# mLSTM gates as eight columns of the value projection, x's mean square per token, and a new order of loads and S5 phases in a decoder layer

## The reference, cut to what matters

```python
def rms_norm(x, g):
    y = xf * lax.rsqrt(jnp.mean(xf * xf, axis=-1, keepdims=True) + RMS_EPS)
    return y * g

p = rms_norm(x, norm_pre_mix) @ w_in     # columns: S5 256 | mLSTM 4*256 + 8 | RWKV 1024 | MoBA 768

# mlstm_mixer
q, k, v, o, i_pre, f_pre = split_cols(p, (GW, GW, GW, GW, nh, nh))     # i_pre, f_pre: 4 + 4 columns
log_i = i_pre + i_bias
bcum = cumsum(log_sigmoid(f_pre + f_bias))    # within a chunk
...
# s5_mixer: diagonal complex recurrence, its phases are cos and sin of t * angle
# cross-attention: memory is normed by its own mean square
```

## Time and profile before

| | |
|---|---|
| median of 3 runs | 482.74 us |
| the profiled execution | 482.97 us, its span (first to last instruction) 481.2 us |
| PE busy | 471.1 us (98%), 3330 matmuls |
| VectorE busy | 345.4 us (72%), 488 instructions |
| ScalarE busy | 270.6 us (56%), 442 instructions |
| GpSimd busy | 108.4 us (23%), 75 instructions |
| chain that ended last | PE 70%, VectorE 19%, issue 3%, ScalarE 3%, DMA 2% |
| granted PE clock | 0.998 of full speed |

### The profile page before, as it was taken

One profiled execution on the slowest core, in us unless ns is written; L12 is line 12 of the kernel. 1 busy time (PEld: TensorE's weight loads), 2 busy tenths in 40 slices (PEclk: granted clock), 3 DMA queues, 4 the chain that ended last, 5 costly groups with the idle time before them and its releaser, 6 DMA issues.

```text
span 481.2 us, 8231 instructions
## 1 busy us (share of the span) xinstructions
PE 471.1 (98%) x3330; PEld 409.0 (85%) x3330; DVE 345.4 (72%) x488; ACT 270.6 (56%) x442; POOL 108.4 (23%) x75
## 2 busy tenths in 40 slices
PE   8999999999999999999999999999999999999995
PEld 6999888989888877889998887888888888888884
DVE  3899999999889887888455736767676777642234
ACT  5678884417232347679557556655555555453342
POOL 0005427793576600000000000000000000344450
PEclk9999999999999999999999999999999999999999
DMA  7874429221410226263733532465555455455502
GB/s 267 338 314 168 161 89 340 69 99 50 148 71 20 89 89 262 86 246 123 260 116 133 207 143 88 176 218 185 196 209 198 176 176 185 172 194 217 193 0 87
DMA packets 12697, 78.91 MB, mean 164 GB/s; under 512 B 1487, under 2 KB 2164, under 8 KB 4084
## 3 DMA queue, kind: packets, MB, share of 16 engines
q1 hardware_dynamic: 12660, 78.39, 45.4%
HBM read 77.33 MB, written 1.84 MB: 165 GB/s over the span
## 4 chain that ended last, share of the span: by engine, by line
PE 70%; DVE 19%; issue 3%; ACT 3%; DMA 2%; POOL 1%; SPq 1%; DVEq 0%; ACTq 0%
PE bank L414 69%; DVE we_rest L385 3%; DMA ring<-weights 2%; POOL arena L1166 1%; DVE arena L1742 1%; DVE wm_rest L385 1%; DVE bank L1689 1%; ACT we_high L379 1%; ACT arena L1440 1%; DVE arena L2014 1%; DVE wk_rest L385 1%; DVE h L1945 0%; DVE arena L397 0%; DVE arena L1759 0%; DVE arena L1879 0%
## 5 line engine op out<-in xcount | busy, mean ns | idle before, releaser
L414 PE MATMUL bank<-h,w_high 128*128 128x512 f32 (+1 forms) x392 | 120.4, 372 | 0.0
L379 ACT ACTIVATE w_high<-ring 128x1024 fp32r<-128x1024 f32 x63 | 66.2, 1058 | 62.7 <-PE bank L414 59.2
L385 DVE TENSOR_TENSOR w_rest<-ring,w_high 128x1024 fp32r<-128x1024 f32 x51 | 63.3, 1245 | 49.2 <-ACT w_high L379 49.0
L414 PE MATMUL bank<-h,w_rest 128*128 128x256 f32 x320 | 89.6, 280 | 0.0
L414 PEld LDWEIGHTS bank<-h,w_high 128*128 128x128 f32 x392 | 68.7, 188 | 13.6 <-issue 0.4
L385 POOL TENSOR_TENSOR w_rest<-ring,w_high 128x1024 fp32r<-128x1024 f32 x7 | 16.8, 2400 | 259.5 <-ACT w_high L379 259.5
L414 PEld LDWEIGHTS bank<-h,w_rest 128*128 128x128 f32 x320 | 60.5, 189 | 0.0
L414 PE MATMUL bank<-arena 64*64 64x64 f32 (+8 forms) x794 | 51.3, 253 | 1.6 <-POOL arena L1119 1.1
L385 DVE TENSOR_TENSOR w_rest<-third_slot,w_high 128x1024 fp32r<-128x1024 f32 x27 | 32.7, 1222 | 27.3 <-ACT w_high L379 27.2
L414 PEld LDWEIGHTS bank<-arena 64*64 64x64 f32 (+4 forms) x794 | 42.2, 144 | 11.4 <-issue 3.9
L414 PE MATMUL bank<-h,we_high 128*128 128x256 f32 x256 | 47.2, 287 | 2.1 <-DVE we_rest L385 1.6
(11 more groups left out here) (341 smaller groups left out, 1020.2 us busy)
## 6 DMA issues: line engine op xcount, KB each, us to landing
ring<-weights SPq DMA_DIRECT2D x49, 1024.0 KB, 4.8
third_slot<-weights SPq DMA_DIRECT2D x15, 1024.0 KB, 4.8
gain<-gains SPq DMA_DIRECT2D x3, 512.0 KB, 5.6
cst<-consts SPq DMA_DIRECT2D x1, 1216.0 KB, 8.8
par<-params SPq DMA_DIRECT2D x1, 1168.0 KB, 10.4
kx<-x_t SPq DMA_DIRECT2D x2, 512.0 KB, 5.6
ring<-weights SPq DMA_DIRECT2D x2, 512.0 KB, 6.6
vx<-mem_t SPq DMA_DIRECT2D x1, 1024.0 KB, 9.7
```

The lines of the kernel that those rows point to most:

```text
L379: nc.scalar.activation(split_half(i)[0], raw_half(i), ACT.Copy).then_inc(S["w_high"], 1)
L385: e.tensor_tensor(rest_, raw_half(i), high.bitcast(F32), ALU.subtract).then_inc(rest_done(i)[0], 1)
L414: return nc.tensor.matmul(out_, lhsT, rhs, start=start, stop=stop, skip_group_check=True)
```

## The change

The 8 gate columns are loaded as a 1024 x 8 matrix, split into high and rest, and stored behind the 256 value columns (`w_gated`); the value product of a token block is 264 columns wide, each block in its own bank. ScalarE copies the 8 columns, scaled, to `gate_cols`, and PE turns them (two transposes) between the halves of ml_o. x's mean square comes from x's rows (tokens on partitions), loaded now before slot 2: two squares with a sum, the root in one column, two diagonal matrices, and PE spreads them over partitions with ones (`rstd_x`). Memory squared follows the shift of rw_v; the sines are built ahead of rests(6); rests(9) and highs(9) go ahead of the theta subtraction and of the shift of rw_r. The identity and time constants join the first constants; the other constants and the later parameters load before slot 6. Nothing else is changed but memory places (Vt and BKt swapped, a memset of `gate_cols`).

```diff
@@ pe @@
+            def values_and_gates(n, names, banks, act):
+                for name, b in zip(names, banks):
+                    pe_open(pe, name, b)
+                pe.wait_ge(S["gate_split"], 4)
+                for j in range(2):
+                    wait_rest(pe, 2 * n + j)
+                    for m in range(2):
+                        o = bank[banks[m]][:, 0:256 + GATES]
+                        for k in range(4):
+                            kt = 4 * j + k
+                            last = mm3(o, [x[:, kt, m * P:(m + 1) * P] for x in act],
+                                       [x[:, k, :] for x in w_gated[j]], kt == 0, kt == KD - 1)
...
             split_channel_major(1, "rw_k", 0, h_split, None, (0,))
-            o = pe_open(pe, "x_sumsq", 2)
-            pe.wait_ge(S["ones_in"], 16)
-            pe.wait_ge(S["x_summed"], 3)
-            mm(o[:, 0:T], const("ones"), sq_x[:, 0, :])
+            o = pe_open(pe, "rstd_x", 2)
+            pe.wait_ge(S["x_diag"], 2)
             for m in range(2):
-                last = mm(o[:, T + m:T + m + 1], sq_x[:, 0, m * P:(m + 1) * P], const("ones")[:, 0:1])
+                last = mm(o[:, m * P:(m + 1) * P], const("ones"), x_diag[:, m, :])
...
-            pe.wait_ge(S["consts_in"], 16)          # before rw_w; now before rw_kk
...
             split_channel_major(6, "ml_k", 1, h_split)
-            o = pe_open(pe, "gates", 2)
-            pe.wait_ge(S["gate_gain"], 1)
-            for k in range(KD):
-                last = mm(o[0:GATES, 0:T], v3(prm("w_gate"), GATES)[:, k, :], hT[:, k, :], k == 0, k == KD - 1)
-            last.then_inc(full[2], 1)
             moved(pe, "s5_u")
+            pe.wait_ge(S["more_params_in"], 16)
...
-            split_values(7, "ml_v", 0, h_split)
-            split_channel_major(8, "ml_o", 1, h_split)
+            values_and_gates(7, ("ml_v0", "ml_v1"), (0, 2), h_split)
+            split_channel_major(8, "ml_o", 1, h_split, None, (0,))
+            o = pe_open(pe, "gates", 7)
+            moved(pe, "ml_v0")
+            moved(pe, "ml_v1")
+            for m in range(2):
+                last = nc.tensor.transpose(o[0:GATE_ROWS, m * P:(m + 1) * P], gate_cols[:, m, 0:GATE_ROWS], const("ident"))
+            last.then_inc(full[7], 1)
+            split_channel_major(8, "ml_o", 1, h_split, None, (1,))
@@ sp @@
                 if n == 2:
                     sp.dma_start(cst[:, 0:CONST_FIRST], consts_d[:, 0:CONST_FIRST]).then_inc(S["ones_in"], 16)
-                if n == 3:
-                    sp.dma_start(cst[:, CONST_MORE:], consts_d[:, CONST_MORE:]).then_inc(S["consts_in"], 16)
+                    for m in range(2):
+                        sp.dma_start(xres[:, m, :], x_rows[m * P:(m + 1) * P, :]).then_inc(S[f"xres{m}_in"], 16)
                 if n == 4:
-                    sp.dma_start(par[:, PARAM_FIRST:], params_d[:, PARAM_FIRST:]).then_inc(S["params_in"], 16)
+                    sp.dma_start(par[:, PARAM_FIRST:PARAM_MORE], params_d[:, PARAM_FIRST:PARAM_MORE]).then_inc(S["params_in"], 16)
...
+                if n == 6:
+                    sp.dma_start(cst[:, CONST_MORE:], consts_d[:, CONST_MORE:]).then_inc(S["consts_in"], 16)
+                    sp.dma_start(par[:, PARAM_MORE:], params_d[:, PARAM_MORE:]).then_inc(S["more_params_in"], 16)
                 if n == S_WKV:
-                    sp.dma_start(xres, x_rows.rearrange("(m p) c -> p m c", p=P)).then_inc(S["xres_in"], 16)
@@ act @@
             highs(2)
-            x_square(0)
+            a.activation(step, prm("log_step"), ACT.Exp).then_inc(S["s5_step"], 1)
             highs(4)
-            x_square(1)
-            a.activation(step, prm("log_step"), ACT.Exp).then_inc(S["s5_step"], 1)
+            for m in range(2):
+                act.wait_ge(S[f"xres{m}_in"], 16)
+                x_square(m)                      # Square of xres[:, m, :] with accum_out=ssq[:, m]
+            a.activation(rstd_col, ssq[:, 0:2], ACT.Ln, bias=const("eps6"), scale=1.0 / D).then_inc(S["sq_ready"], 1)
+            act.wait_ge(S["sq_ready"], 3)
+            a.activation(rstd_col, rstd_col, ACT.Exp, scale=-0.5).then_inc(S["rstd_col"], 1)
+            act.wait_ge(S["rstd_col"], 1)
+            for m in range(2):
+                a.activation(x_diag[:, m, :], const("ident"), ACT.Copy, scale=rstd_col[:, m:m + 1]).then_inc(S["x_diag"], 1)
...
             highs(6)
-            inv_root("x_sumsq", rstd_x, T, 1.0 / D, "eps6").then_inc(S["rstd_x"], 1)
+            a.activation(rstd_x, o[:, 0:T], ACT.Copy).then_inc(free_of("rstd_x"), 1)
...
+            highs(9)
             shifted("rw_r", 2)
             highs(10)
             a.activation(cos, sin, ACT.Abs).then_inc(S["sincos"], 1)
+            shifted("rw_v", 3)
             a.activation(sq_m, mem_h, ACT.Square).then_inc(S["sq_m_ready"], 1)
-            shifted("rw_v", 3)
             highs(12)
+            for j in range(2):
+                a.activation(w_gated[j][0][:, :, 256:256 + GATES], raw_gates(j), ACT.Copy).then_inc(S["gate_split"], 1)
...
-            a.activation(rows[0][0:NH, :], o[32:32 + NH, 0:T], ACT.Identity, bias=prm("f_bias", NH))
...
             highs(H_MID + 2)
-            project_values("ml_v", mlv)
+            gated_values(0, "ml_v0")             # 8 columns to gate_cols, then 256 to mlv, both scaled
+            gated_values(1, "ml_v1")
+            o = wait_full(act, "gates")
+            a.activation(rows[0][0:NH, :], o[32:32 + NH, 0:T], ACT.Identity, bias=prm("f_bias", NH))
@@ dve @@
             rests(4)
-            dve.wait_ge(S["sq_ready"], 2)
-            sum_tiles(dve, v, sq_x, "x_summed")
...
-            rests(6)
-            x_scale("rw_wag")
-            dve.wait_ge(S["consts_in"], 16)
+            dve.wait_ge(S["ones_in"], 16)
             for i in range(8):
                 last = v.tensor_scalar(sin[:, i, :], const("time"), frac[:, i:i + 1], None, ALU.mult)
+            rests(6)
+            x_scale("rw_wag")
...
             x_scale("rw_r")
+            rests(9)
             v.scalar_tensor_tensor(sin, cos, ROUND, sin, ALU.subtract, ALU.subtract).then_inc(S["theta"], 1)
-            rests(9)
...
             rests(12)
-            v.tensor_tensor(w_gate, w_gate, spread(prm("pre_mix"), GATES), ALU.mult).then_inc(S["gate_gain"], 1)
...
             rests(13)
+            for j in range(2):
+                v.tensor_tensor(rest_, raw_gates(j), high.bitcast(F32), ALU.subtract).then_inc(S["gate_split"], 1)
...
-            x_scale("gates", GATES, 1)
...
+            dve.wait_ge(S["consts_in"], 16)      # before the masks of A0 to A7
```

More of the change, by code:

```diff
@@ L23 @@
 DFF = 2816
-GATES = 36
+GATES = 2 * NH
+GATE_ROWS = 36
 NFF = DFF // P
@@ L212, in trunk_kernel @@
             own(stage, "gap", A_AT)
-            w_early = [pair(stage, f"we{i}", HALF, 256) for i in range(HALF_BUFS)]
+            w_early = [pair(stage, f"we{i}", HALF, 256) for i in range(2)]
+            w_gated = [pair(stage, f"we{i}", 4 * (256 + GATES), 256 + GATES) for i in range(2, HALF_BUFS)]
+            w_early += [[x[:, :, 0:256] for x in w] for w in w_gated]
         xtmp = v3(own(ctx, "xtmp", 2 * D), D)
@@ L319, in wait_slot @@
             return slot(n)
-        SCALED = ["rw_wag", "rw_k", "rw_r", "rw_v", "ml_q", "ml_k", "gates", "ml_o"]
+        SCALED = ["rw_wag", "rw_k", "rw_r", "rw_v", "ml_q", "ml_k", "ml_o"]
         def scaled(eng, name):
@@ L483, in split_values @@
                     used(last, i, name if j else None)
+            def values_and_gates(n, names, banks, act):
[3 more added lines that the diff above has]
+                for j in range(2):
+                    i = 2 * n + j
+                    wait_rest(pe, i)
+                    for m in range(2):
[4 more added lines that the diff above has]
+                                       [x[:, k, :] for x in w_gated[j]], kt == 0, kt == KD - 1)
+                        if j == 1 and m == 0:
+                            last.then_inc(full[banks[0]], 1)
+                    used(last, i, names[1] if j else None)
             def split_wide_values(halves, names, banks, act, parts):
@@ L845, in _ @@
             moved(pe, "qk3")
-            moved(pe, "ml_v")
+            moved(pe, "ml_v1")
             attend("num", 2, mlv, E)
@@ L1360, in _ @@
             act.wait_ge(S["rw_E"], 1)
-            project_values("ml_v", mlv)
+            gated_values(0, "ml_v0")
+            gated_values(1, "ml_v1")
+            o = wait_full(act, "gates")
+            a.activation(rows[0][0:NH, :], o[32:32 + NH, 0:T], ACT.Identity,
+                         bias=prm("f_bias", NH)).then_inc(S["ml_gate"], 1)
+            a.activation(rows[1][0:NH, :], o[0:NH, 0:T], ACT.Identity, bias=prm("i_bias", NH)).then_inc(free_of("gates"), 1)
             act.wait_ge(S["ml_gate"], 1)
@@ L1683, in x_rest, with x_scale @@
                     e.then_inc(S["h_rest"], 1)
-            def x_scale(name, rows_=P, n=2):
-                dve.wait_ge(S["rstd_x"], 1)
```

(13 more changed lines are left out.)

58 lines of the change are left out of this document (32 added, 26 removed).

## The result

| | before | after |
|---|---|---|
| median of the runs (4 each) | 483.0 us (482.57 to 483.32) | 485.52 us (485.06 to 486.35) |
| ratio | | 1.0055, 95% interval 1.0043 to 1.0067 |
| the profiled execution, its span | 482.97, 481.2 | 485.8, 484.0 |
| PE busy | 471.1 | 470.6 |
| VectorE busy | 345.4 | 342.9 |

A forecast was written before the change was run, and what follows sets the result against it. VectorE's queue up to the first mask was taken as the bound, PE's savings becoming waits. Kk's scaling 0.3, less 0.2 for gate splits, plus 0.3 for gates' scaling, gave 0.4 us off: 482.3 us, range 480.4 to 484.0.

The forecast's parts named there:

- What bounds in the first 80 us: 10 to 80 us: PE and VectorE run neck and neck; only a shorter VectorE queue up to the first mask helps.
- the two places named: PE's saving turns into waits at ml_v (half 14) and at ml_o's bank, two holes of 2 us or more.
- Rival (b): All that PE saves shows, VectorE's holes being closed: 4.4 us off, 478.3 us; chance 0.11.
- The costs on paper: First 80 us: PE 4.4 us ahead by 74 us; VectorE sheds 3.5 us and gains 0.2 for two gate splits.
- Step 1 and 2: Loads, then ScalarE's squares and root: x's rows and slot 2 in by 18.8 us, high 4 starts at 19.0.
- Rival (c): x's rows and slot 2 land late, high 4 at 20.7, later work shifts by 1.7 us: 484.0 us; chance 0.12.
- Step 4: Rests 10 and 11 take turns with GpSimd's sum, started at 38.5 as before; kk's scaling begins 0.3 us sooner.
- Rival (d): PE's clock falls to 1.2 GHz after the two new holes, slowing ml_o and a second stretch: 486 us; chance 0.05.
- From that point all later work moves together.: After the first mask, the 0.4 us won is carried unchanged to the kernel's end.
- rest 10's turn as a limit: Rest 10, ready at 39.4, gains nothing: its turn beside GpSimd comes at 40.9, and rest 11 ends at 44.1.
- Step 3: VectorE to the theta step, ending at 33.9; the 2 us won are lost as it waits from 37.6 till 39.4.

The follow-up runs named there:

- e7: The kernel before with one of the eight f32 gate products on PE in place of eight; 483.16 us, ratio 1.0001.
- e1: The changed kernel with 224 unused columns behind the parameters, so every later tile lies at its old place; 483.77 us, ratio 1.0012.
- e3: The changed kernel with tiles at their old places and four products of zeros before each of PE's two standstills; 483.5 us, ratio 1.0006.
- e10: The changed kernel with old tile places, x's rows loaded late and the squares reading x's channel-major copy; 482.85 us, ratio 0.9998.
- e2: The changed kernel with four small products of zeros before each of PE's two standstills; 485.39 us, ratio 1.0046.
- e6: The changed kernel with 224 unused columns behind h: h at the new place, feed-forward weights at the old; 484.86 us.
- e8: The changed kernel with old tile places and ScalarE's highs 10 and 11 ahead of memory squared, no products of zeros; 481.72 us, ratio 0.9977.
- e9: The kernel before with ScalarE's shift of rw_v and highs(12) ahead of memory squared; 482.41 us, ratio 0.9989.
- e11: The kernel before with 32 unused columns behind the middle weights: h keeps its place, feed-forward weights move up 128 bytes; 484.25 us.
- e4: The changed kernel with old tile places, the products of zeros, and highs 10 and 11 ahead of memory squared; 481.9 us, ratio 0.9974.
- e5: The kernel before with 32 unused columns (128 bytes) behind the parameters, moving every later tile; 485.24 us.
- e11 to e16: e11, then five runs of the kernel before with everything behind the parameters 256, 40, 64, 168 or 192 bytes further; 482.72, 485.62, 485.12, 484.97, 484.83 us.

## Why the prediction was wrong, point by point

- **What bounds in the first 80 us.** Right: PE's 3.4 us became waits at the two places named, and e7 gained nothing by 3.1 us of saved matmuls. Rival (b) is dead.
- **The costs on paper.** Right: the 264-column matmuls are 0.12 us apart (60.66 to 66.44 for 48), the two gate splits take 0.28 (forecast 0.2, bound 0.6), kk's scaling was held back (1.09), x's diagonals met PE as said. The whole from high 4 to the first mask, 57.0 us in four profiles, is what the steps gave (76.1 less 19.0 is 57.1).
- **Step 1 and 2, the start of high 4.** This term was mis-sized. The sum gave 19.0; the profiles have 19.5 to 20.4. One reason was named (x's rows ahead of slot 2, behind ScalarE's wait), with an upper bound of 1.4 us, but the value taken was the rate of a full microsecond, 426 GB/s, kept up without a pause; e1 and e3 waited 0.7 us for slot 2 at that point. By e10 the rows cost an estimated 0.7 us in the median. In `after` itself no such wait is seen: of its 0.6 us beyond 19.0, 0.2 are slot 1 (13.4 for 13.2) and 0.4 a distance of 6.2 us from there to high 4, where the steps gave 5.8. Rival (c) said that the gain is gone from a start at 19.4, and the six of the table are all later; its mechanism is seen in part, at less than half of its 1.7 us in the mean.
- **Step 4, the shared stretch.** The turns were right: rest 11 ends 5.7 us behind GpSimd's start, before and after. But that start was at 39.4, 0.8 later than before, where I had it level; this is the late high 4 again.
- **Rival (d), the clock.** It happened: a fall to the 1.2 GHz level for 3 us behind the second hole, in the place named. The price was overstated: I priced two slow stretches and took off PE's lead of 2 us only once, which made 3.7 us over the forecast. The profiles have one fall each, behind the first hole no consumer waits for it, and e2 and e3 give an estimated 0.3 to 0.4 us. The rule of the Trainium skill ("TensorE: Matmul & The Clock Gate", HAM oscillation — how this bites in real kernels) that gaps send the engine back to half rate is borne out by the falls in after, e1, e6, e7, e8 and e10. That the kernel comes out at (d)'s 486 for it is not.
- **"From that point all later work moves together."** This sentence was the error that decides the sign. 2.0 of the 2.65 us lie behind 313 us, in matmuls that the diff doesn't touch, and come from the 896 bytes by which a smaller `w_gate` moves all later tiles. The diff showed the column count falling from 36 to 8, and I read it as a saving only. No part of the sum and no rival had a term for it. With the tiles at their old place (e1, 483.77) the time would have been inside the range, still 1.5 us above the forecast of 482.3; some 0.3 of this is the kernel before itself, whose median is 483.0 with the fourth run and was 482.74 in the forecast.
- **The shared stretch as a chance.** I had rest 10's turn as a limit. The Trainium skill's rule ("SBUF — State Buffer", Who interferes with whom) that whoever issues first holds the shared pair and the other blocks is what e8 and e9 show: 2.36 for two rests when they are first, 4.80 when GpSimd is, and the block passes to whatever instruction stands next (2.80 for 0.69, 2.71 for 0.6). I used it to price the change. Step 3 had even named the idle time ("waits till 39.4"), and I didn't see that one moved line would put it to use.

Account by the ratios: 2.65 us = 2.1 for the place (1.0055 against 1.0012), 0.7 for x's rows loaded early (1.0012 against 0.9998), and 0.1 below nothing for all else, which includes both the savings and the clock. Each difference of two ratios is uncertain by some 0.7 us. The place is shown, and by the ruler it is 2.0; the 0.7 is barely clear of nothing, and what the clock has in the rest stays open.

## What to carry to other kernels

When a change alters the size of any tile, the tiles behind it move; compare the mean duration of an untouched group of matmuls before and after, and if it differs, pad the tile back before judging the change. Work taken off an engine that isn't alone in setting the end is worth nothing until the other engine's list gets shorter, and the standstills it leaves can lower the clock. Where two engines share ports, a new order moves the hold to another instruction but need not shorten it; look for idle time just ahead of the shared stretch, and bring work forward into it.

## What the runs showed of the hardware that I had not expected

- A pair of a 512-column and a 256-column fp32r matmul takes 346.7 or 353.3 ns by the place of its tiles (within 256 bytes, as seven places suggest), and 351.0 if only one of the two operands is moved from the fast place (e6, e11). The fast place isn't an aligned one. Not every group shows it: the 80 `w_rest,act_high` matmuls of 512 columns have a mean of 389 ns in before, after and all the shifted kernels. With only one operand moved a smaller group is slower too (the 32 `w_rest,h` of 512 columns: 390 ns before, 394 in e6, 393 in e11). What in the hardware makes it isn't settled by these runs.
- In all six profiles in which PE had a standstill of 1.9 us or more between 10 and 80 us the clock fell to about 0.50 for about 3 us: in some executions behind the first (1.9 us in e1, e6, e10), in some behind the second (1.9 and 1.9 in after, 1.0 and 2.3 in e7, 1.6 and 1.9 in e8). Four small products of zeros in each were enough to keep it at 1.00 (e2, e3, e4). Before the change, waits of up to 1.0 us never did it.
- The landing of the first slots varies by about 1 us between executions of like kernels: slot 1's highs start at 12.7 to 13.9 in ten profiles of the old order (before, e5, e7, e9, e11 to e16) and at 13.1 to 13.9 in eight of the new. High 4 follows with 17.8 to 18.7 and, with the rows early, 19.1 to 20.4. A forecast from the landings of one profile is no sharper than that.
